# Arrays in the slab begin at word 80 in place of word 48, in a two-block transformer kernel

## The chip, the cores and the metric

The kernel runs on one core of a Trainium2 chip. The metric is the device time of one execution in microseconds (us). All arrays named below lie in the on-chip memory (SBUF), which has 128 partitions; a "word" is four bytes of one partition, so an array that begins 32 words further begins 128 bytes further in every partition.

## The reference

Two stacks follow one another on 256 tokens of width 1024. The first block has two hybrid layers (a state-space mixer, latent attention, a gated delta rule, gates, and a squared-ReLU feed-forward net); the second, with 256 further context tokens, has one neighbourhood-attention layer and one gated linear recurrence, each with a SwiGLU net. What takes nearly all the arithmetic is the products with the weights:

```python
proj = xn @ w_in                                   # 1024 -> 9472
q = rmsnorm(cq, q_norm_g) @ w_uq ; kv = rmsnorm(ckv, kv_norm_g) @ w_ukv
mixed = g_ssd * (y_ssd @ w_ssd_out) + g_mla * (y_mla @ w_mla_out) + g_gdn * (y_gdn @ w_gdn_out)
h = x + mixed @ w_out
f = jnp.square(jax.nn.relu(rmsnorm(h, norm2_g) @ w_up)) @ w_down
...
q, k, v = jnp.split(h @ w_qkv, 3, axis=-1)         # second block
(jax.nn.silu(a) * u) @ w_out                       # a, u = h @ w_in
```

All is float32. These products are called the dense stages here.

## The kernel before

**Memory.** One float32 tensor, the slab, has 34720 words (`ARENA`) and holds the arrays of both blocks, one block after the other in the same place. An `Arena` hands out consecutive pieces of it; `A.at` is the next free word. Each block sets `A.at = SHIFT` (L411, L469) before its first large array, and the first block, after some small arrays, rounds up to the next word that is `SHIFT` modulo 256 (L422). Every large array has a multiple of 256 words, so each row of 256 tokens in the slab begins at word `SHIFT` modulo 256. Behind the slab, from word 34720 on, lies the ring: four pairs of slots of 1024 words for the raw weights and the low halves of the weights, and two pairs for the high halves (`rounded`, L372, L373). Word 34720 is word 160 modulo 256. A stationary tile of weights has 128 words, so weight tiles begin at word 32 or 160 modulo 256. Constants and the residual `x2` lie behind the ring.

**Dense stages.** A float32 factor is split in a high and a low part (type fp32r), and a product is three matmuls into the same place of PSUM: high weights by high activations, high by low, low by high (L955, L956, L957 in `dense`; L993 to L995 in `lead`, the first tiles of a job; L1036 to L1038 in `rows`). In `dense` and `lead` a 128 x 128 tile of weights is stationary, and the activations move: 256 columns of them, or 512 where both token sets of the second block go together (`xh, xl = v[:, k, 0:n]`). In `rows` the roles are the other way: a tile of activations is stationary, and the weights move, 256 columns in two pieces of 128 (or 512 in one). Every matmul has its own load of a stationary tile, which the trace shows on a line of its own (PEld), ahead of the matmul that uses it.

**Where operands begin.** Activations begin at word 48 modulo 128 and weights at word 32 modulo 128, whatever the tile or the layer. The other matmuls (attention, chunked recurrences, transposes) are float32, not split, and most of their operands are in the slab too.

**Order.** Each engine has one program, written out by generators that `order1` and `order2` interleave. Loads of the weights go through SP's queue, one MB each. ScalarE rounds the raw weights to the high part (L1592), VectorE subtracts for the low part (L2261, some on GpSimd, L3162), and TensorE takes them in the order of `weights`.

Of the kernel before, what the change touches and what calls it, by code (L numbers as in the profile page):

```python
# [14 lines left out]
T = 256  # L15
NEG = -1e30
ARENA = 34720
SHIFT = 48
SLOT = 1024
RAW = 4  # L20
HI = 4
# [143 lines left out]
class Shared:  # L165
# [243 lines left out]
    def block1_memory(self):  # L409
        A = Arena(self.slab)  # L410
        A.at = SHIFT  # L411
        self.xn = self.pair(A, 8, T)
# [8 lines left out]
        self.ea = self.slab[:, A.at - 32:A.at - 8]  # L421
        A.at += (SHIFT - A.at) % 256  # L422
        keep = A.at
# [42 lines left out]
    def block2_memory(self):  # L466
        A = Arena(self.slab)
        self.A1, self.A2, self.FA = A(8, 2), A(8, 2), A(8)
        A.at = SHIFT  # L469
        self.h = self.pair(A, 8, 512)  # L470
# [2991 lines left out]
```

## Time and profile before

| | us |
|---|---|
| median of 3 runs | 2435.35 |
| lowest and highest | 2431.0, 2436.66 |
| the profiled execution | 2436.84 |
| its span, first to last instruction | 2435.1 |
| TensorE busy in it | 2374.2 (97%) |
| VectorE, ScalarE, GpSimd busy | 1436.2, 1248.7, 281.4 |
| granted TensorE clock, mean | 0.992 |

Outside the span lie 1.7 us. Matmuls are pipelined: one is shown for longer than the time from its start to the next one's start, so the time that one costs is read from starts. The granted clock is full (2.4 GHz) but for the first stages.

### The profile page before, as it was taken

How to read it: one execution, taken by the hardware profiler on the slowest of the kernel's cores; microseconds unless marked ns; L12 is line 12 of the kernel's file. 1: busy time of each engine (PE TensorE's matmuls, PEld its weight loads, DVE VectorE, ACT ScalarE, POOL GpSimd, SP SyncE). 2: the span in 40 equal slices, each digit the busy share in tenths (PEclk: the TensorE clock that was granted, in tenths of full speed). 3: DMA queues.
4: the chain of work that ended last, by engine and by line, in shares of the span. 5: the costliest groups of instructions: out<-in, count | busy, mean ns of one | idle time of the engine just before them, and what ended most of it. 6: DMA issues, size and time to landing. Idle time of an engine off the chain costs nothing.

```text
span 2435.1 us, 48140 instructions
## 1 busy us (share of the span) xinstructions
PE 2374.2 (97%) x21314; PEld 2206.5 (91%) x21314; DVE 1436.2 (59%) x2147; ACT 1248.7 (51%) x1845; POOL 281.4 (12%) x163
## 2 busy tenths in 40 slices
PE   8989999999999899999999999999999999998999
PEld 8979899999999798999999886887889998788999
DVE  6773876665567467766655347643335554776554
ACT  6746656554476465466543367542224444355443
POOL 4203000000041310001010014200000001330000
PEclk9999999999999999999999999999999999999999
DMA  5344445555444444445553245333225542223554
GB/s 220 139 157 161 150 176 188 177 190 191 171 168 148 151 155 155 173 177 205 184 183 120 104 153 194 126 120 136 104 104 191 192 158 101 92 83 128 190 190 157
DMA packets 56128, 381.00 MB, mean 156 GB/s; under 512 B 6256, under 2 KB 9840, under 8 KB 10736
## 3 DMA queue, kind: packets, MB, share of 16 engines
q1 hardware_dynamic: 55024, 374.59, 43.0%
q8 instruction: 168, 2.75, 0.5%
q10 hardware_dynamic: 896, 3.33, 0.4%
q14 instruction: 40, 0.33, 0.0%
HBM read 375.80 MB, written 1.05 MB: 155 GB/s over the span
## 4 chain that ended last, share of the span: by engine, by line
PE 81%; DVE 10%; ACT 7%; issue 2%; POOL 0%; DMA 0%; ACTq 0%; SPq 0%; DVEq 0%; POOLq 0%
PE ps L955 21%; PE ps L957 21%; PE ps L956 21%; DVE r L2261 3%; ACT r L1592 2%; PE ps L1036 1%; PE ps L1037 1%; PE ps L1038 1%; PE ps L993 1%; PE ps L994 1%; PE ps L995 1%; PE ps L914 1%; PE ps L1094 1%; PE ps L876 1%; DVE slab L2347 1%
## 5 line engine op out<-in xcount | busy, mean ns | idle before, releaser
L955 PE MATMUL ps<-r,r 128*128 128x256 f32 (+1 forms) x4448 | 1318.5, 296 | 9.7 <-DVE slab L2347 2.2
L956 PE MATMUL ps<-r,r 128*128 128x256 f32 (+1 forms) x4448 | 1304.4, 293 | 0.0
L957 PE MATMUL ps<-r,r 128*128 128x256 f32 (+1 forms) x4448 | 1303.9, 293 | 0.0
L2261 DVE TENSOR_TENSOR r<-ring,r 128x1024 fp32r<-128x1024 f32 (+1 forms) x562 | 685.0, 1249 | 435.2 <-ACT r L1592 433.4
L955 PEld LDWEIGHTS ps<-r,r 128*128 128x128 f32 x4448 | 835.3, 188 | 45.6 <-issue 11.2
L957 PEld LDWEIGHTS ps<-r,r 128*128 128x128 f32 x4448 | 835.5, 188 | 22.2
L956 PEld LDWEIGHTS ps<-r,r 128*128 128x128 f32 x4448 | 835.7, 188 | 21.8 <-issue 0.5
L1592 ACT ACTIVATE r<-ring 128x1024 fp32r<-128x1024 f32 (+1 forms) x610 | 613.3, 1041 | 169.7 <-PE ps L957 149.4
L3209 POOL TENSOR_TENSOR slab<-slab 128x512 f32<-128x512 f32 (+1 forms) x20 | 28.7, 1436 | 1210.0 <-ACT slab L1708 1190.7
L3162 POOL TENSOR_TENSOR r<-ring,r 128x1024 fp32r<-128x1024 f32 x48 | 114.2, 2402 | 236.2 <-ACT r L1592 236.1
L2347 DVE SCALAR_TENSOR_TENSOR slab<-ps,v,slab 128x255 f32<-128x255 f32 (+1 forms) x168 | 67.8, 473 | 64.1 <-ACT slab L1660 64.1
L1733 ACT ACTIVATE r<-slab 128x512 fp32r<-128x512 f32 x33 | 20.9, 632 | 137.8 <-DVE slab L2416 137.8
L993 PE MATMUL ps<-r,r 128*128 128x256 f32 x288 | 83.8, 291 | 7.0 <-DVE r L2913 2.5
L994 PE MATMUL ps<-r,r 128*128 128x256 f32 x288 | 81.4, 283 | 0.0
L995 PE MATMUL ps<-r,r 128*128 128x256 f32 x288 | 81.3, 282 | 0.0
L1036 PE MATMUL ps<-r,r 128*128 128x256 f32 (+1 forms) x272 | 79.4, 292 | 0.0
L1037 PE MATMUL ps<-r,r 128*128 128x256 f32 (+1 forms) x272 | 77.4, 284 | 0.0
L1038 PE MATMUL ps<-r,r 128*128 128x256 f32 (+1 forms) x272 | 77.4, 284 | 0.0
L1729 ACT ACTIVATE slab<-ps 128x512 f32<-128x512 f32 x33 | 19.8, 599 | 96.8 <-PE ps L957 94.6
L1708 ACT ACTIVATE slab<-x 128x512 f32<-128x512 f32 x36 | 22.7, 630 | 87.8 <-DVE x L2392 50.5
L1680 ACT ACTIVATE slab<-ps 128x512 f32<-128x512 f32 (+1 forms) x50 | 29.4, 587 | 72.2 <-PE ps L957 72.0
L3251 POOL TENSOR_TENSOR slab<-slab,posi 128x768 f32<-128x768 f32 (+1 forms) x24 | 38.6, 1609 | 223.3 <-DVE posi L2986 223.3
(357 smaller groups left out, 2559.6 us busy)
## 6 DMA issues: line engine op xcount, KB each, us to landing
ring<-in_win SPq DMA_DIRECT2D x73, 1024.0 KB, 4.8
ring<-in_ada SPq DMA_DIRECT2D x48, 1024.0 KB, 4.8
ring<-in_fi SPq DMA_DIRECT2D x44, 1024.0 KB, 4.7
ring<-in_fo SPq DMA_DIRECT2D x36, 1024.0 KB, 4.8
ring<-in_wup SPq DMA_DIRECT2D x32, 1024.0 KB, 4.7
ring<-in_wdn SPq DMA_DIRECT2D x32, 1024.0 KB, 4.8
ring<-in_hin SPq DMA_DIRECT2D x20, 1024.0 KB, 4.8
ring<-in_nqkv SPq DMA_DIRECT2D x12, 1024.0 KB, 4.7
```

Of the source, the lines that this page charges most:

```text
L955: self.mm(o, hi[:, k - k0, cs], xh, k == 0, False)
L956: self.mm(o, hi[:, k - k0, cs], xl, False, False)
L957: i = self.mm(o, lo[:, k - k0, cs], xh, False, k == last)
L993: self.mm(o, hi, xh, k == 0 and t % per == 0, False, skip_group_check=True)
L994: self.mm(o, hi, xl, False, False, skip_group_check=True)
L995: i = self.mm(o, lo, xh, False, k == kt - 1, skip_group_check=True)
L1036: self.mm(o, xh, cut(hi, k), k == 0, False)
L1037: self.mm(o, xh, cut(lo, k), False, False)
L1038: i = self.mm(o, xl, cut(hi, k), False, k == kt - 1)
L1592: self.act(K.high(p), K.raw(p), ACT.Copy).then_inc(*self.up("w_hi", p))
L2261: self.tt(K.low(p), K.raw(p), K.high(p).bitcast(F32), ALU.subtract).then_inc(*self.up("w_lo_v", p))
L3162: self.tt(K.low(p), K.raw(p), K.high(p).bitcast(F32), ALU.subtract).then_inc(*self.up("w_lo_g", p))
```

## The change

One constant. Both blocks' first large array begins at word 80 of the slab in place of word 48, the rounding at L422 goes to word 80 modulo 256, and so all large arrays begin 32 words further. The three small arrays of the second block that are handed out before `A.at = SHIFT` stay. The slab's size, the ring, the constants, `x2` and all PSUM places stay, and each engine has the same instructions in the same order.

```diff
 ARENA = 34720
-SHIFT = 48
+SHIFT = 80
 SLOT = 1024
```

In the built programs the operands of the 18397 matmuls differ so: in 14344 the moving operand alone begins 128 bytes further (these are `dense`, `lead` and some others), in 1400 the stationary one alone (`rows` is among them), in 2149 both, and in 504 none. No output in PSUM moves.

| matmuls | moving minus stationary, before, in words modulo 128 | after |
|---|---|---|
| `dense`, `lead` | 48 - 32 = 16 | 80 - 32 = 48 |
| `rows` | 32 - 48 = 112 | 32 - 80 = 80 |

## Rows read from the trace of the kernel before

**Rows 1.** The page: engines' busy time; then their busy tenths, and the clock.

```profile
PE 2374.2 (97%) x21314; PEld 2206.5 (91%) x21314; DVE 1436.2 (59%) x2147; ACT 1248.7 (51%) x1845; POOL 281.4 (12%) x163
...
PE   8989999999999899999999999999999999998999
...
PEclk9999999999999999999999999999999999999999
```

**Rows 2.** The page: the chain that ended last, share of the span by engine and line.

```profile
PE 81%; DVE 10%; ACT 7%; issue 2%; POOL 0%; DMA 0%; ACTq 0%; SPq 0%; DVEq 0%; POOLq 0%
PE ps L955 21%; PE ps L957 21%; PE ps L956 21%; DVE r L2261 3%; ACT r L1592 2%; PE ps L1036 1%; PE ps L1037 1%; PE ps L1038 1%; PE ps L993 1%; PE ps L994 1%; PE ps L995 1%; PE ps L914 1%; PE ps L1094 1%; PE ps L876 1%; DVE slab L2347 1%
```

**Rows 3.** Groups by line and shape, PE: xcount | busy us, mean ns | idle before.

```profile
L955 PE MATMUL ps<-r,r 128*128 128x256 f32 x3904 | 1102.3, 282 | 9.7 <-DVE slab L2347 2.2 <-DVE r L2315 2.2 <-DVE r L2261 2.0
...
L955 PE MATMUL ps<-r,r 128*128 128x512 f32 x544 | 216.2, 397 | 0.0
...
L993 PE MATMUL ps<-r,r 128*128 128x256 f32 x288 | 83.8, 291 | 7.0 <-DVE r L2913 2.5 <-DVE r L2261 2.1 <-DVE r L2469 1.4
...
L1036 PE MATMUL ps<-r,r 128*128 128x256 f32 x256 | 72.9, 285 | 0.0
...
L1036 PE MATMUL ps<-r,r 128*128 128x512 f32 x16 | 6.5, 409 | 0.0
```

**Rows 4.** One line in one stretch: L955 from 480 to 640 us; then 340 to 365.

```profile
engine op xcount: duration ns min/median/max, first and last start us, forms
L955 PE MATMUL ps<-r,r x454: 279/279/279, 479.8 to 639.9; 128*128 128x256 f32 x152
...
L955 PE MATMUL ps<-r,r x71: 280/280/280, 339.9 to 364.7; 128*128 128x256 f32 x71
```

**Rows 5.** Busy time by stretch: PE, PEld, DVE, ACT, POOL, then clock, DMA share, GB/s.

```profile
480.00:490.00 10.00, 10.00 (x87) 10.00 (x86) 6.86 (x8) 6.10 (x8) 0.00 (x0) 1.00 0.61 211
...
590.00:600.00 10.00, 10.00 (x87) 10.00 (x86) 3.76 (x4) 4.11 (x4) 0.00 (x0) 1.00 0.48 184
```

**Rows 6.** As rows 4: L955, 256 columns, from 1039.5 us; then from 818.2 us.

```profile
L955 PE MATMUL ps<-r,r x15: 276/276/276, 1039.4 to 1044.2; 128*128 128x256 f32 x15
...
L955 PE MATMUL ps<-r,r x15: 276/276/276, 818.2 to 823.0; 128*128 128x256 f32 x15
```

**Rows 7.** As rows 4: L1037, in `rows`, in five stretches.

```profile
L1037 PE MATMUL ps<-r,r x31: 281/281/283, 1389.8 to 1400.4; 128*128 128x256 f32 x31
...
L1037 PE MATMUL ps<-r,r x30: 276/276/277, 1404.9 to 1414.8; 128*128 128x256 f32 x30
...
L1037 PE MATMUL ps<-r,r x32: 281/281/283, 1418.9 to 1429.8; 128*128 128x256 f32 x32
...
L1037 PE MATMUL ps<-r,r x15: 276/276/277, 1434.0 to 1438.8; 128*128 128x256 f32 x15
...
L1037 PE MATMUL ps<-r,r x124: 276/276/276, 1981.0 to 2022.8; 128*128 128x256 f32 x124
```

**Rows 8.** As rows 4: L955 with 512 columns, in two stretches.

```profile
L955 PE MATMUL ps<-r,r x175: 392/392/394, 1710.4 to 1829.9; 128*128 128x512 f32 x175
...
L955 PE MATMUL ps<-r,r x31: 388/388/397, 1640.8 to 1661.4; 128*128 128x512 f32 x31
```

**Rows 9.** Chain that ended last, in time order, float32 matmuls: start us, us, what.

```profile
332.63 3.46 PE ps L1094 x16
...
382.65 3.46 PE ps L1370 x16
...
1386.42 3.43 PE ps L1094 x8
```

**Rows 10.** As rows 4: VectorE's L2261, whole span, and who waited for it.

```profile
L2261 DVE TENSOR_TENSOR r<-ring,r x562: 946/1224/2651, 9.0 to 2424.9; 128x1024 fp32r<-128x1024 f32 x180, 128x768 fp32r<-128x768 f32 x8
...
  PE ps L955: 2.0, 6
```

## The prediction

> **What bounds the kernel now.** I read four things, in this order. First the busy shares: TensorE is busy for 2374.2 of 2435.1 us and in nearly every slice [rows 1], so all its idle time together is 61 us. Second the chain that ended last: 81% is TensorE, and L955 to L957 alone are 63% [rows 2]. Third the groups: the split products are 3 x (3904 + 288 + 256) = 13344 matmuls of 256 columns and 3 x (544 + 16) = 1680 of 512 columns [rows 3] (each line has two sisters with the same count). Fourth, what one of them costs, which is the distance between starts and not the shown duration. L955 occurs every third matmul: 454 of them from 479.8 to 639.9 us are 160.1 / 453 / 3 = 0.1178 us each, and 71 from 339.9 to 364.7 us are 24.8 / 70 / 3 = 0.118 [rows 4]. With 512 columns it is 119.5 / 174 / 3 = 0.2289 us in one stretch and 20.6 / 30 / 3 = 0.229 in another [rows 8]. So the split products take about 13344 x 0.1175 + 1680 x 0.231 = 1568 + 388 = 1956 us, 80% of the span. Only this spacing is large enough for an edit that moves nothing but addresses.
>
> The reader is to see that the spacing is nobody else's doing. In ten microseconds with VectorE busy for 6.86, ScalarE for 6.10 and DMA at 0.61 there are 87 matmuls, and in ten with 3.76, 4.11 and 0.48 there are 87 too [rows 5]. It is not the bare streaming rate either. Float32 matmuls, which are not split, take 3.46 / 16 = 216 ns for 256 columns and 3.43 / 8 = 429 ns for 512 [rows 9]. If a split one took half of that, as its columns come twice as fast, it would be 108 and 214 ns; these are my estimates from those rows. Against them a dense matmul loses 9.8 ns with 256 columns and 15 ns with 512. Something about two streams (moving columns, next stationary tile) costs this at the full rate and not at half of it.
>
> And the loss has levels. Some stretches of the same line, with operands at the same places modulo 256 words, run faster: 15 matmuls of L955 from 1039.4 to 1044.2 us, and the same from 818.2 to 823.0, each shown with 276 ns where the long stretch has 279 and 280 [rows 4, 6]. The start times to two decimals allow 4.8 / 14 / 3 = 0.114. The `rows` stage gives the level better: 41.8 / 123 / 3 = 0.1133 us for 124 of L1037, shown with 276 ns, and 10.6 / 30 / 3 = 0.1178 for 31 shown with 281 [rows 7]. A stretch keeps its level from its first matmul to the next interruption. By the start times in the timeline, about 960 of the 13344 matmuls are at the low level: 535 of about 745 in `rows` (72%) and 430 of about 12,300 in `dense` and `lead` (3.5%). The distance between the two levels is 4.4 ns.
>
> **The change, part by part.** It removes no instruction, wait or transfer, and adds none.
>
> Instructions on VectorE, ScalarE and GpSimd: the same counts, with operands 128 bytes further. The costliest group, L2261, reads and writes the ring, which stays; TensorE waited 2.0 us in all for it at L955 [rows 10]. The rest work on the slab at a multiple of 64 bytes before and after. I take 0. If a tenth of the 17% of the chain that is VectorE's and ScalarE's [rows 2] changed by 1% either way, it would be 0.4 us.
>
> Float32 matmuls outside the split products: L1094 (slab moving, constants stationary) and L1370 (both in the slab) have one spacing, 216 ns, at two different distances of their operands [rows 9]. At half rate the place does not show, so 0.
>
> `dense` and `lead`: the moving operand goes from 16 to 48 words past the stationary one, modulo 128. `rows`: from 112 to 80. No row of before shows the distances 48 or 80, so the cost is bounded from both sides. Below: every matmul at the estimated bare rate, which takes away (117.5 - 108) x 13344 = 127 us and (231 - 214) x 1680 = 29 us, 156 in all. Above: the levels are 4.4 ns apart, and one further level on the 12,400 that are at the high one, and two on the 960, is 4.4 x 14,300 = 63 us; a 256-column matmul that lost what a 512-column one loses (15 ns in place of 9.8) gives 5.2 x 13344 = 69 us, nearly the same.
>
> Between these ends I take 0, for one reason in the rows. `rows` and `dense` have operands at quite different distances (112 and 16), with roles exchanged, and yet their two levels are the same to a tenth of a nanosecond, 117.8 and 113.3 [rows 4, 7]. What they share is the distance modulo 32 words: 16 in both. The change is exactly 32 words, so that keeps its 16. Whatever alternates with a period of 32 words or less, or not at all, can't tell the two kernels apart. A dependence on the distance in larger units would have to give both stages the same two levels by chance.
>
> The Trainium skill speaks to this on its page "SBUF — State Buffer", section "Who interferes with whom": TensorE has two read ports, one for the moving operand and one for the stationary load, that are independent. By that rule a change of the distance is worth nothing, and the same sum of 0 comes out; but its page "TensorE: Matmul & The Clock Gate", section "Back-to-back issue gap", puts 256 columns at 256 / 2.4 + 2.5 = 109.2 ns, and the trace has 117.8, so something that these rules don't name is at work, and I don't count them as evidence for 0.
>
> The sum: 2436.84 us of the profiled execution, plus 0. The median of the runs is 1.5 us below that execution; I forecast the median, 2435.4.
>
> **The rivals.**
>
> *Dense takes the mix of `rows`.* If the distance counts modulo 64 words, the edit exchanges the two stages: `dense` had 16 and gets 48, and `rows`, which had 112, that is 48, gets 16. For this speaks that `rows` begins at the low level much more often, 72% of its matmuls against 3.5% [rows 6, 7]. Against it: `rows` also differs in its moving pattern (two pieces of 128) and its count of stretches is only seven, of which three are at the high level. Price: 12,300 x (0.72 - 0.035) x 4.4 ns = 37 us gained, and up to 535 x 4.4 ns = 2 us lost in `rows`: 2400 us.
>
> *The loss goes away.* The two streams would no longer meet. That is the lower bound, 2435 - 156 = 2279 us. Against it: two distances have been seen, and neither avoids the loss.
>
> *The loss grows (slower).* If places count modulo 128 words, 48 and 80 are new, and the next stationary tile could meet the moving columns more often. Place: every split product, and the wait is inside the matmul, so nothing hides it; TensorE has 61 us of idle in all, and what waits for others would take up only a part. Price: the whole further level 63 to 69 us, so 2435 + 66 = 2501 us; if only some stretches, or the 512-column ones (another 4.4 ns x 1680 = 7 us) take it, something from 2441 to 2475. It decides against me as soon as the mean spacing of 256 columns is over 0.1179 us in place of 0.1175, since 0.4 ns x 13344 is 5 us.
>
> *The edit does what it says but only the starts are shuffled.* All 960 low-level matmuls at the high level would be 960 x 4.4 ns = 4 us more: 2439.5, still within 0.2%.
>
> **How the numbers follow.** No change of the levels, shuffled starts included: 0.54, of which 0.02 fall on each side of 0.2%. The mix of `rows`: 0.14. The loss goes away or halves: 0.06. The loss grows in part: 0.14; wholly: 0.12. So faster by over 0.2% has 0.22, within 0.2% 0.50, slower by over 0.2% 0.28. A measurement of this kernel tells about 0.2%, that is 5 us, from no change. The likeliest case has its own range of 2429 to 2442. The range for 8 in 10 has to take in the mix of `rows` (2400, down to 2394 if a little more of `dense` goes low) and most of the further level: 2394 to 2490. It leaves out the vanishing loss and the full further level, together 0.18.
>
> **What would show it.** In the profile of the changed kernel the long stretch of L955 from 480 to 640 us should again hold 454 starts at 279 ns shown, and the 512-column one 175 starts in 119.5 us. Right for the mix of `rows`: most stretches of L955 at 276 ns shown and 0.1133 spacing, and L1037 now mostly at 281. Right for growth: 283 ns or more shown and a spacing near 0.122. The float32 lines L1094 and L1370 should stay at 216 ns in each case; if they move, the cause is not the one argued here. My step is wrong if either of `dense` or `rows` shows a third level, since that is a dependence on more than the place within 32 words.

## The result

| | before | after |
|---|---|---|
| median of 5 runs, us | 2435.35 | 2419.82 |
| lowest and highest | 2431.0, 2436.82 | 2413.3, 2422.75 |
| ratio, 95% interval | | 0.9931 (0.9918 to 0.9945) |
| span of the profiled execution | 2435.1 | 2419.6 |

The changed kernel is faster by 0.7%, 15.5 us. Within 0.2% was forecast. The time lies in the stated range, but the forecast of no change was wrong.

Times and ratios are of runs with a mean granted clock of 0.988 or more; one run of `b1_80` (3306.78 us, clock 0.653) and one of `best` (3678.68 us, clock 0.585) ran at a lower one and are left out.

The page of the kernel after shows TensorE busy for 19 us less, its weight loads for 26 us less, and the other three engines as they were, within 1 us [rows 1]:

```profile
span 2419.6 us, 48140 instructions
...
PE 2355.6 (97%) x21314; PEld 2180.4 (90%) x21314; DVE 1437.0 (59%) x2147; ACT 1249.1 (52%) x1845; POOL 280.8 (12%) x163
...
PE 80%; DVE 10%; ACT 7%; issue 2%; POOL 0%; DMA 0%; SPq 0%; DVEq 0%; ACTq 0%; POOLq 0%
```

Where it went shows in one line in one stretch, as in [rows 4, 7, 8]; the columns are count, shown duration in ns (min/median/max), and the first and last start in us. First L955 with 256 columns, in three stretches:

```profile
L955 PE MATMUL ps<-r,r x471: 276/276/276, 479.9 to 639.7; 128*128 128x256 f32 x157
...
L955 PE MATMUL ps<-r,r x298: 281/281/281, 1134.7 to 1239.7; 128*128 128x256 f32 x149
...
L955 PE MATMUL ps<-r,r x71: 281/281/281, 416.0 to 440.7; 128*128 128x256 f32 x71
```

The long stretch from 480 us held 454 starts before [rows 4] and holds 471 now: 159.8 / 470 / 3 = 0.1133 us each. That is the low level that [rows 6] had in a few short stretches. The other two stretches are still at the high one, 105.0 / 297 / 3 = 0.1178. Then L1037 in `rows` (against [rows 7]), and L955 with 512 columns (against [rows 8]):

```profile
L1037 PE MATMUL ps<-r,r x29: 280/280/280, 1394.0 to 1403.9; 128*128 128x256 f32 x29
...
L1037 PE MATMUL ps<-r,r x119: 279/279/279, 1970.0 to 2011.7; 128*128 128x256 f32 x119
...
L955 PE MATMUL ps<-r,r x176: 393/398/499, 1701.0 to 1823.6; 128*128 128x512 f32 x176
...
L955 PE MATMUL ps<-r,r x30: 393/396/398, 1631.0 to 1651.3; 128*128 128x512 f32 x30
```

The stage `rows`, which was at 0.1133 for 124 starts of L1037 in its last stretch, is at 41.7 / 118 / 3 = 0.1178 now, in every stretch. And with 512 columns a matmul costs 122.6 / 175 / 3 = 0.2335 and 20.3 / 29 / 3 = 0.2333 us, where it was 0.229: that stage lost. The float32 matmuls did not move, as the chain of waits shows (start us, us, what; the columns of [rows 9]):

```profile
332.06 3.45 PE ps L1094 x16
...
380.90 3.46 PE ps L1370 x16
...
1375.53 3.43 PE ps L1094 x8
```

Summed over all distances between starts of split matmuls in the two traces:

| | before, mean ns | after, mean ns | all of them, us |
|---|---|---|---|
| `dense`, `lead`, 256 columns (12,300) | 117.6, 3.5% low | 115.0, 62% low | -25.5 |
| `dense`, 512 columns (1570) | 229.1 | 233.3 | +6.5 |
| `rows`, 256 columns (755) | 114.7, 72% low | 117.8, none low | +2.4 |
| `rows`, 512 columns (44) | 233.2 | 229.6 | -0.1 |
| all else on TensorE | | | +1.3 |
| sum | | | -15.4 |

"Low" is the share of matmuls at the low level. The means leave out the first matmul of a stretch and those behind a wait; the sums have them. The span fell by 15.5. The granted clock does not set the two levels apart: from 480 to 640 us it was 1.00 before and after. So `dense` and `rows` have exchanged their behaviour, with 256 columns and with 512.

### The profile page after: what moved, and what is told of

Its sections match the earlier page's. It is cut to its first block, busy times and chain, and to the rows that moved or that the text cites. A ratio compares the mean times of both kernels' runs of the same rounds, so it can differ in the third digit from the quotient of the medians.

```text
span 2419.6 us, 48140 instructions
## 1 busy us (share of the span) xinstructions
PE 2355.6 (97%) x21314; PEld 2180.4 (90%) x21314; DVE 1437.0 (59%) x2147; ACT 1249.1 (52%) x1845; POOL 280.8 (12%) x163
## 4 chain that ended last, share of the span: by engine, by line
PE 80%; DVE 10%; ACT 7%; issue 2%; POOL 0%; DMA 0%; SPq 0%; DVEq 0%; ACTq 0%; POOLq 0%
PE ps L955 21%; PE ps L957 21%; PE ps L956 21%; DVE r L2261 3%; ACT r L1592 2%; PE ps L1036 1%; PE ps L1037 1%; PE ps L1038 1%; PE ps L914 1%; PE ps L1094 1%; PE ps L876 1%; PE ps L993 1%; PE ps L995 1%; PE ps L994 1%; PE ps L1463 1%
## 5 line engine op out<-in xcount | busy, mean ns | idle before, releaser
L955 PE MATMUL ps<-r,r 128*128 128x256 f32 (+1 forms) x4448 | 1317.1, 296 | 11.0 <-DVE r L2261 2.8
L957 PE MATMUL ps<-r,r 128*128 128x256 f32 (+1 forms) x4448 | 1301.9, 293 | 0.6 <-issue 0.6
L956 PE MATMUL ps<-r,r 128*128 128x256 f32 (+1 forms) x4448 | 1302.2, 293 | 0.0
L2261 DVE TENSOR_TENSOR r<-ring,r 128x1024 fp32r<-128x1024 f32 (+1 forms) x562 | 685.8, 1251 | 429.9 <-ACT r L1592 428.4
L955 PEld LDWEIGHTS ps<-r,r 128*128 128x128 f32 x4448 | 840.2, 189 | 49.4 <-issue 11.3
L956 PEld LDWEIGHTS ps<-r,r 128*128 128x128 f32 x4448 | 839.9, 189 | 24.5 <-issue 0.8
L957 PEld LDWEIGHTS ps<-r,r 128*128 128x128 f32 x4448 | 839.4, 189 | 24.5
L3162 POOL TENSOR_TENSOR r<-ring,r 128x1024 fp32r<-128x1024 f32 x48 | 114.0, 2399 | 233.2 <-ACT r L1592 233.1
L1037 PE MATMUL ps<-r,r 128*128 128x256 f32 (+1 forms) x272 | 77.8, 286 | 0.0
```

The costliest lines, as they stand in the source:

```text
L955: self.mm(o, hi[:, k - k0, cs], xh, k == 0, False)
L956: self.mm(o, hi[:, k - k0, cs], xl, False, False)
L957: i = self.mm(o, lo[:, k - k0, cs], xh, False, k == last)
L1037: self.mm(o, xh, cut(lo, k), False, False)
L2261: self.tt(K.low(p), K.raw(p), K.high(p).bitcast(F32), ALU.subtract).then_inc(*self.up("w_lo_v", p))
L3162: self.tt(K.low(p), K.raw(p), K.high(p).bitcast(F32), ALU.subtract).then_inc(*self.up("w_lo_g", p))
```

## The experiments

The median of the kernel before on the same chip stood between 2434.7 and 2437.7 us in all of them. In the table, "distance" is the place of the slab's large arrays minus that of the weight tiles in words modulo 64, which for `rows` has the opposite sign. The means and shares are from the start times of `dense` and `lead`, and of one execution of each kernel, the profiled one. For `s144` that was the slowest of seven (2433.53 us, where the others took 2415.96 to 2425.4).

| kernel | distance | median us | ratio (95%) | 256 columns, ns (low share) | 512 columns, ns |
|---|---|---|---|---|---|
| before | 16 | 2435.35 | 1 | 117.6 (3.5%) | 229.1 |
| after | 48 | 2419.82 | 0.9931 (0.9918 to 0.9945) | 115.0 (62%) | 233.3 |
| `ring32` | 48 | 2423.74 | 0.9941 (0.9923 to 0.9958) | 115.6 (50%) | 233.3 |
| `ring32_80` | 16 | 2437.06 | 1.0011 (0.9999 to 1.0024) | 117.5 (7%) | 229.3 |
| `s112` | 16 | 2436.01 | 0.9995 (0.9985 to 1.0006) | 117.4 (9%) | 229.0 |
| `s144` | 48 | 2420.45 | 0.9943 (0.9922 to 0.9965) | 115.7 (48%) | 233.3 |
| `s96` | 0 | 2457.45 | 1.0085 (1.0070 to 1.0100) | 119.9 (0%) | 227.1 |
| `s64` | 32 | 2457.70 | 1.0092 (1.0071 to 1.0113) | 119.0 (0%) | 232.4 |
| `s72` | 40 | 2453.01 | 1.0068 (1.0051 to 1.0084) | 118.0 (0%) | 234.3 |
| `s88` | 56 | 2449.78 | 1.0050 (1.0035 to 1.0065) | 118.3 (0%) | 233.3 |

**Is it the distance between the operands, or the place of the activations?** Theory A was the distance modulo 64 words, theory B the activations' place alone. Two kernels with the ring 32 words earlier:

```diff
-ARENA = 34720
+ARENA = 34688
 SHIFT = 48
```

> Slab arrays at word 48 as before; slab 32 words shorter (34688), so the ring and all that lies behind it begin 32 words earlier. Weight tiles then begin at word 0 modulo 128, the moving activations at 48: distance 48, the one of the changed kernel, with the moving operand where it was before. Theory A, the distance of moving to stationary operand modulo 64 words decides: as the changed kernel, 2420 us, most stretches of L955 with 256 columns at 0.1133 us spacing (276 ns shown), with 512 columns 0.2333, and L1037 with 256 columns at 0.1178 (281 ns shown). Theory B, the place of the activations alone decides: as before, 2435 us, L955 nearly all at 0.1178, L1037 mostly at 0.1133.

The second has `SHIFT = 80` too.

> Slab arrays at word 80, ring 32 words earlier: distance 80, that is 16 modulo 64. Theory A (distance modulo 64 words): as before, 2435 us, L955 with 256 columns nearly all at 0.1178 us, with 512 columns 0.229 to 0.231, L1037 mostly 0.1133. Theory B (place of the activations alone): as the changed kernel, 2420 us.

`ring32` took 2423.74 us and `ring32_80` 2437.06. L955 in each, from 480 and from 1712 us:

```profile
L955 PE MATMUL ps<-r,r x472: 276/276/276, 479.8 to 639.9; 128*128 128x256 f32 x158
...
L955 PE MATMUL ps<-r,r x162: 281/396/398, 1712.0 to 1824.7; 128*128 128x512 f32 x161, 128*128 128x256 f32 x1
```

```profile
L955 PE MATMUL ps<-r,r x454: 279/279/279, 479.8 to 639.9; 128*128 128x256 f32 x152
...
L955 PE MATMUL ps<-r,r x165: 392/392/394, 1712.3 to 1824.9; 128*128 128x512 f32 x165
```

The first fence is `ring32`: activations where they were before, and the counts of the changed kernel. The second is `ring32_80`: activations where the changed kernel has them, and the very counts of before (454 starts, 279 ns). Theory B fell. What decides is the relative place of the two operands. One part of the second expectation missed: in `rows` 29% of the matmuls were at the low level, not most of them (72% before). The last stretch of `rows`, 384 matmuls, took the high level here and the low one before, at the same distance modulo 64, so that the share of a few stretches is partly a matter of how each one starts.

**What is its period?** `SHIFT = 112` and `SHIFT = 144`, ring as before:

> Slab arrays at word 112, ring as before: distance 80 modulo 128 words. Theory A with a period of 64 words: as before, 2435 us, with 512 columns at 0.229 to 0.231. Theory C, the distance counts modulo 128 or more: a spacing or a mix that neither kernel has, over 5 us away from 2435.

> Slab arrays at word 144: distance 112 modulo 128, that is 48 modulo 64. Theory A: as the changed kernel, 2420 us, 512 columns at 0.2333 to 0.2354. Theory C: something else by over 5 us.

2436.01 and 2420.45 us. The line L955, first in `s112` and then in `s144`, in the same stretches:

```profile
L955 PE MATMUL ps<-r,r x453: 279/279/279, 480.1 to 639.8; 128*128 128x256 f32 x151
...
L955 PE MATMUL ps<-r,r x165: 392/392/392, 1712.1 to 1824.7; 128*128 128x512 f32 x165
```

```profile
L955 PE MATMUL ps<-r,r x472: 276/276/276, 479.8 to 639.9; 128*128 128x256 f32 x158
...
L955 PE MATMUL ps<-r,r x162: 393/396/398, 1712.1 to 1824.8; 128*128 128x512 f32 x162
```

80 modulo 128 acts as 16, and 112 as 48. Every pair that agrees modulo 64 words (256 bytes) agrees with 512 columns to 0.3 ns. Theory C fell.

**What lies between 16 and 48?** `SHIFT` 64, 96, 88 and 72:

> Slab arrays at word 64: moving minus stationary is 32 modulo 64 in the dense stages and 32 in rows too. Distances so far: 16 gives 0.1178 us nearly throughout with 256 columns and 0.2291 with 512; 48 gives half to two thirds of the matmuls at 0.1133 and 0.2333. Theory A1, the cost runs smoothly between them: between 2420 and 2435 us, 512 columns between 0.229 and 0.2333. Theory A2, only distances half way (0 or 32) let the two streams miss each other: below 2410, a spacing under 0.1133 or 0.229. Theory A3, they collide most there: above 2440, a spacing over 0.1178 or 0.2333.

> Slab arrays at word 96: distance 0 modulo 64, for dense and rows alike. Theory A1 (smooth between 48 and 16): between 2420 and 2435 us. Theory A2: below 2410. Theory A3: above 2440; the two streams would then start in the same place.

> Slab arrays at word 88: distance 56 modulo 64, 8 words past the changed kernel's. Steps of 8 words tell whether the period of 64 words has a finer place in it. If only the half of the period decides (32 to 63 against 0 to 31): as the changed kernel, 2420 us, 512 columns 0.2333. If every step counts: more than 5 us away.

> Slab arrays at word 72: distance 40 modulo 64, 8 words short of the changed kernel's. If only the half of the period decides: 2420 us, 512 columns 0.2333. If every step counts: more than 5 us away, and on the other side from distance 56.

All four are slower than both kernels, by 0.5 to 0.9% against before. L955 in `s96`, with 256 columns and then with 512:

```profile
L955 PE MATMUL ps<-r,r x445: 282/283/283, 479.9 to 639.7; 128*128 128x256 f32 x149
...
L955 PE MATMUL ps<-r,r x147: 389/389/389, 1730.3 to 1829.5; 128*128 128x512 f32 x147
```

With 256 columns this is a third level, 159.8 / 444 / 3 = 0.1200 us. With 512 columns the same distance is the cheapest of all, 99.2 / 146 / 3 = 0.2265. So A3 was right on the time for 0 and 32, and wrong on what a distance does: there is no distance that is good or bad as such, it depends on the width. Half a period does not decide either: 40 and 56 lie on the two sides of 48, both are slower than it by about 30 us, and both lie on the same side in time, against what the last expectation had.

**Do the terms add up by stage?** `b1_80` has its own `SHIFT1 = 80` for the first block and 48 for the second. `best` has in addition the hidden activations of the second block 32 words further:

```diff
+SHIFT1 = 80
...
-        A.at = SHIFT
+        A.at = SHIFT1
...
-        A.at += (SHIFT - A.at) % 256
+        A.at += (SHIFT1 - A.at) % 256
...
-            A.at = early
+            A.at = early + SHIFT1 - SHIFT
```

The last pair of lines is in `best` alone.

> One half of the change: the first block's arrays at word 80, the second block's at 48. The changed kernel's gain with 256 columns is 16 us in the first block by the spacings of the two traces, and its losses (512 columns, 7 us, and rows in the second block, 2.5 us) are all in the second. If the terms add up stage by stage: 2435 - 16 = 2419 us, 512 columns back at 0.229 to 0.231 us, block-one stretches of L955 mixed between 0.1133 and 0.1178. If the level is a property of a whole execution and not of the stage's distance, the second block changes too.

> As the kernel with only the first block at word 80, and in the second block the hidden activations (moving with 256 columns alone) 32 words further too, while h, which moves with 512 columns, stays at 48. By the terms measured: another 6 us with 256 columns, so 2435 - 16 - 6 = 2413 us, the lowest of all; if the level at the start of a stretch is drawn anew, 2410 to 2420.

`b1_80` took 2423.85 us (ratio 0.9954, 0.9940 to 0.9968), 5 us more than forecast. Stage by stage it did what was expected: 512 columns are back at 229.0 ns, `rows` at 114.3 with 80% low, and the first block's stretches are mixed. It has 39% of all the 256-column matmuls at the low level. `best` took 2423.01 us (0.9953, 0.9936 to 0.9970), against 2413 forecast. It has 39% too. Its last long stretch, on L956 in this kernel (L955 of before, one line further down), begins with the up-projection, whose activations are still at distance 16, and goes over at 2360 us, without an interruption, into the down-projection at distance 48:

```profile
L956 PE MATMUL ps<-r,r x512: 277/280/301, 2241.1 to 2421.7; 128*128 128x256 f32 x171
```

That is 180.6 / 511 / 3 = 0.1178 us, and it is 117.8 ns in each of the two parts: the level with which the stretch began went on at the new distance. So the price by stage is right for 512 columns and uncertain for 256: at distance 48 a stretch may take either level. This same stretch (1536 matmuls) ran at 113.3 ns in the changed kernel and at 117.8 in `ring32` and `s144`, all three at distance 48; the difference is 1536 x 4.5 ns = 7 us.

**What comes of two distances at once?** In `hi32` the slab is as before, and the high tiles alone lie 32 words further:

```diff
-        self.ring = self.sb("ring", [128, (2 * RAW + HI) * SLOT])
+        self.ring = self.sb("ring", [128, (2 * RAW + HI) * SLOT + 32])
...
-        self.highs = [self.rounded(ARENA + 2 * (RAW + i) * SLOT, 2 * SLOT) for i in range(HI // 2)]
+        self.highs = [self.rounded(ARENA + 2 * (RAW + i) * SLOT + 32, 2 * SLOT) for i in range(HI // 2)]
```

> Slab at word 48 as before; only the high halves of the weights lie 32 words further (the ring is 32 words longer, and what lies behind it moves too). A high tile is then 48 away from the moving activations modulo 64, a low tile 16. Theory D, the cost arises between the columns that move and the stationary tile that is loaded beside them for the next matmul: with 512 columns a triple costs two times 233.3 and once 229.1, a mean of 231.9 ns, as two of the three loads are of high tiles; in rows, where the weights move, also a mix. Theory E, only the place of the slab against the start of the ring as a whole, or one of the two kinds of tiles, decides: 229.1 or 233.3. With 256 columns: a mix of levels or a new one, between 2420 and 2445 us.

2409.35 us, ratio 0.9896 (0.9879 to 0.9914): the fastest kernel of the study, and faster than both, with four runs between 2408.47 and 2410.81. L955 of `hi32`, in the stretch that the changed kernel had at the high level, in the last long one, and with 512 columns; then what waited for L2261 (us, times), and its chain's shares:

```profile
L955 PE MATMUL ps<-r,r x251: 276/276/276, 1135.0 to 1220.0; 128*128 128x256 f32 x126
...
L955 PE MATMUL ps<-r,r x436: 276/276/384, 2231.8 to 2379.9; 128*128 128x256 f32 x146
...
L955 PE MATMUL ps<-r,r x138: 392/393/394, 1704.6 to 1799.9; 128*128 128x512 f32 x138
...
  PE ps L955: 5.1, 10
...
PE 75%; DVE 13%; ACT 9%; issue 2%; POOL 0%; DMA 0%; SPq 0%; DVEq 0%; ACTq 0%; POOLq 0%
```

96% of the 256-column matmuls of `dense` and `lead` are at the low level, mean 113.6 ns; that is 37 us less than before; 512 columns (231.8 ns) give back 4 us of it and `rows` 2. The mean with 512 columns is what theory D said, 231.9. Its parts are not: L955 has 231.1, L956 229.0 and L957 235.5 ns, where D wanted 233.3, 229.1, 233.3. The place behind L956, beside which the low tile is loaded, is right.

Three more kernels were to tell what makes the low level stay: the two distances exchanged (`SHIFT = 80` in `hi32`), and high tiles kept at 48 with low tiles at 0 or 32:

> Slab at word 80 and the high halves of the weights 32 words further: distances exchanged against the kernel with the slab at 48, high tiles 16 modulo 64 from the moving activations, low tiles 48. Theory D for 512 columns (each matmul pays by the tile that is loaded beside it): a triple is 229.1 + 233.3 + 229.1, mean 230.5 ns, the dear one being L956, beside which the low tile is loaded. With 256 columns: if a mix of the two distances is what brings the low level nearly everywhere (96% of matmuls with high 48, low 16), this kernel has it too, 2405 to 2412 us. If it is two of three loads at 48 that do it, most go back to 0.1178: 2425 to 2437 us.

> High tiles 48 from the moving activations modulo 64, low tiles 0 (slab at word 96, high halves 16 words further). If the distance of the high tiles settles the low level with 256 columns: over 80% at 0.1133 us, 2405 to 2415 us; with 512 columns a mean of (2 x 233.3 + 227.1) / 3 = 231.2 ns by theory D. If the low tile at a distance that is dear by itself (0 gave 119.9 ns with 256 columns) counts for its third: (2 x 113.4 + 119.9) / 3 = 115.6 ns, 2430 us.

> High tiles 48, low tiles 32 (slab at word 64, high halves 48 words further). Theory D: with 512 columns (2 x 233.3 + 232.4) / 3 = 233.0 ns. With 256 columns, if the high tiles settle the level: over 80% at 0.1133, 2410 to 2418 us. If the low tile's own price is added: (2 x 113.4 + 119.0) / 3 = 115.3 ns, 2428 us.

| kernel | high, low tiles | median us | ratio (95%) | 256 columns, ns (low share) | 512 columns, ns: expected, measured |
|---|---|---|---|---|---|
| `hi32` | 48, 16 | 2409.35 | 0.9896 (0.9879 to 0.9914) | 113.6 (96%) | 231.9, 231.8 |
| `hi32_80` | 16, 48 | 2443.64 | 1.0029 (1.0016 to 1.0042) | 117.1 (33%) | 230.5, 229.8 |
| `hi48_lo0` | 48, 0 | 2446.56 | 1.0043 (1.0028 to 1.0057) | 118.2 (1%) | 231.2, 232.5 |
| `hi48_lo32` | 48, 32 | 2450.16 | 1.0055 (1.0037 to 1.0073) | 118.2 (0%) | 233.0, 231.1 |

Neither "any two distances" nor "high tiles at 48" is enough. The additive form of theory D is off by 0.7 to 1.9 ns in these three, and in `hi32_80` the dear matmul was L955 (232.2) and not L956 (228.0). In `hi48_lo0` L955 is at the high level in a stretch that was at the low one in `hi32`:

```profile
L955 PE MATMUL ps<-r,r x454: 281/281/281, 479.8 to 639.8; 128*128 128x256 f32 x152
```

**What sets `hi32` apart** shows in how its stretches go on. Of its 89 stretches of 30 or more matmuls in `dense` and `lead`, 39 are at the high spacing over the nine distances from their third start on (mean over 116 ns), about as many as in the changed kernel (38 of 91). But all 39 are at the low one at their end, and none went the other way. With one distance for all tiles the high spacing lasted: it fell in 0 of 84 such stretches before, 0 of 38 after, 0 of 35 in `ring32` and 0 of 36 in `s144`; in `hi32_80` it fell in 1 of 49. The start of a stretch of 984 in `hi32`, one start in nine (start us, us, what):

```profile
1124.16 0.28 PE L956 MATMUL ps<-r,r 128*128 128x256 f32 x1
...
1125.22 0.28 PE L956 MATMUL ps<-r,r 128*128 128x256 f32 x1
...
1126.24 0.28 PE L956 MATMUL ps<-r,r 128*128 128x256 f32 x1
```

The first nine distances are 1.06 / 9 = 0.1178 us, the next nine 1.02 / 9 = 0.1133. Why these two distances bring that about is open.

**What settles the level of a stretch** with one distance is open too. In the three kernels with distance 48 (after, `ring32`, `s144`) it goes with the first two distances between starts, in stretches of nine or more. With 201 ns and then 117 or 118, 45 of 45 stretches were high; with 201 and then 120, 3 of 3 were low; with 206, 25 of 25 were low, and with 222 and then 120, 18 of 18. Other pairs are mixed: after 305 ns, 21 were high and 11 low. Two starts of stretches in the timeline of the kernel after (start us, us, what):

```profile
116.73 0.38 PE L955 MATMUL ps<-r,r 128*128 128x256 f32 x1
116.95 0.28 PE L956 MATMUL ps<-r,r 128*128 128x256 f32 x1
117.06 0.28 PE L957 MATMUL ps<-r,r 128*128 128x256 f32 x1
...
123.95 0.36 PE L955 MATMUL ps<-r,r 128*128 128x256 f32 x1
124.15 0.28 PE L956 MATMUL ps<-r,r 128*128 128x256 f32 x1
124.27 0.28 PE L957 MATMUL ps<-r,r 128*128 128x256 f32 x1
```

The first (221 ns, then 113) runs on at 0.1133, the second (201, then 118) at 0.1178. That fits two streams that keep the phase in which they started, but no kernel set that phase by itself.

## Why the prediction was wrong

**What bounds the kernel** was read rightly: the distance between starts of the split matmuls, which the other engines don't touch, and its two levels. The table of the result accounts for the whole change with these alone.

**The cost of the float32 matmuls and of the other engines** was taken as 0, and L1094 and L1370 kept 3.43 to 3.46 us. The reading of 216 ns as the price of a float32 matmul is that of one record: the program has 18397 matmuls and the trace 21314 records, since a float32 matmul that is not a transpose stands there twice (L1318 is issued 4 times and stands there 8 times). A whole one of 256 columns takes 432 ns.

**Slips of the working.** It took 231 ns for a 512-column matmul where its own rows have 0.2289 and 0.229 us, so the lower bound is about 3 us too low; the two levels are 4.5 ns apart, not 4.4. Neither moves the forecast. The 109.2 ns that it has from the Trainium skill ("TensorE: Matmul & The Clock Gate", section "Back-to-back issue gap") are there the gap of an isolated matmul, and for a stream of loads and matmuls that section says that both set the spacing; so the 117.8 ns of the trace are not by themselves a sign of something that the section leaves out.

**The step that failed** is "Between these ends I take 0". It argued that `dense` and `rows` have quite different distances and the same two levels, so that the distance beyond 32 words could not count. The two levels are the same, after the change as well. But the argument looked at the values of the levels and passed over how often each was taken, which stands further up in the prediction: 3.5% against 72%. The time is the mean over both. `ring32`, `ring32_80`, `s112` and `s144` put a dependence modulo 64 words in the place of that step: distance 16 gives 229.0 to 229.3 ns with 512 columns and 3 to 9% low with 256, distance 48 gives 233.3 ns and 48 to 62%.

**The rival "dense takes the mix of `rows`"** was the right mechanism, with a chance of 0.14 where it had the one observation that set the stages apart. (Seven stretches are few: at the same distance modulo 64 `rows` had 72% low before, 81% in `s112` and 29% in `ring32_80`.) It said that L955 would be mostly at 276 ns shown and L1037 at the high level, and so it came. Its price was -35 us net, and measured was -15.4. Three terms make up most of the difference: the low share became 62% and not 72%, with part of the gain lost where stretches start (25.5 us in place of 37); `rows` lost 2.4, as priced; and the 512-column matmuls lost 6.5 us, which it had at 0. The last could have been priced: `rows` has 44 matmuls of 512 columns at the other distance, and their 233 ns against 229 in `dense` was in the trace of before.

**"The loss grows"** happened for 48 with 512 columns alone, 4.2 ns and 6.5 us where it had 4.4 ns and 7 us. With 256 columns it is real elsewhere: distance 0 brings the level of 119.9 ns, 2.1 over the high one where I priced 4.4, and 2457 us where I priced 2501. **"The loss goes away"** occurred nowhere. **The shuffled starts** were priced at 4 us for all low stretches. At distance 48 one long stretch alone is worth 7 us (`best`, above). That may be why the changed kernel's runs spread over 9.5 us and those of before over 5.8; as only one execution of each kernel was traced, it is not shown.

## What to carry to other kernels

Where one engine is bound by a stream of like instructions, read how often each spacing occurs and with which operands, not only which spacings there are. If two stages differ in that share and in one property of their operands, that difference is evidence, weak where the stretches are few, and a change that exchanges the property should be given a fair chance to exchange the share. Before an array is moved, price every width that uses it: the place that is best with 256 columns was the dearer one with 512, and the fastest kernel here kept the slab in place and moved only one kind of weight tile.

## What the runs showed of the hardware

- The spacing of fp32r matmuls in a stream, each with its own load, depends on the relative place of the moving operand and the stationary tiles modulo 256 bytes: with 512 columns 227.1, 229.1, 232.4, 234.3, 233.3 and 233.3 ns for distances of 0, 16, 32, 40, 48 and 56 words. The records of float32 matmuls (L1094, L1370) are 216 ns apart with 256 columns (median) before, after, and at distance 0. The Trainium skill, on its page "SBUF — State Buffer", section "Who interferes with whom", has TensorE's two read ports as independent; these runs show that the spacing of fp32r matmuls depends on the places of both operands together. That the two reads collide, and that they do so in the memory itself, is argued, not shown.
- With 256 columns a stretch takes one of two spacings, 113.3 or 117.8 ns, and with one distance for all tiles it keeps it until the next interruption (2 changes in 546 stretches of 30 or more at distances 16 and 48), even across a change from distance 16 to 48 (`best`). At distance 48 either occurs, at 16 nearly always the high one, and at 0 neither, but 119.9; at 32, 40 and 56 the means over nine distances lie between 117.0 and 120.1 ns. With high tiles at 48 and low tiles at 16 (`hi32`) the high one gives way to the low one by the 15th matmul, in 39 of 39 stretches.
- A faster TensorE begins to wait: in `hi32` L955 waited 5.1 us for L2261, where it was 2.0 before [rows 10], and VectorE's share of the chain went from 10 to 13%. That is part of why about 30 us less in split matmuls made the span 26 us shorter.
